# Second RMS norm's root moved behind the up-projection, and the last output pair computed by column halves

## What is computed

```python
def rmsnorm(x, w):
    xf = x.astype(jnp.float32)
    y = xf * lax.rsqrt(jnp.mean(xf * xf, axis=-1, keepdims=True) + EPS)
    return (y * w.astype(jnp.float32)).astype(x.dtype)
...
def conv_glu(h, w_up, conv_w, conv_b, w_down):
    gate, val = jnp.split(jnp.einsum('bsd,df->bsf', h, w_up), 2, axis=-1)
    gate = causal_dwconv(gate, conv_w, conv_b)
    return jnp.einsum('bsf,fd->bsd', jax.nn.gelu(gate, approximate=False) * val, w_down)
...
        x = x + jnp.einsum('bsm,md->bsd', mix, w_out[l])
        h = rmsnorm(x, norm2_w[l])
        x = x + conv_glu(h, ffn_w_up[l], ffn_conv_w[l], ffn_conv_b[l], ffn_w_down[l])
```

## Time and profile before

| | us |
|---|---|
| median of 3 runs | 436.13 |
| lowest and highest run | 435.36 and 436.80 |
| profiled execution, first to last instruction (span) | 434.3 |
| PE busy | 412.1 (95%) |
| DVE busy | 278.3 (64%) |
| ACT busy | 247.6 (57%) |

### The profile page before, as it was taken

The page is one execution under the profiler, slowest core; times in us unless marked ns, Lnnn a source line. Parts: engine busy times, 40 slices in busy tenths (PEclk is TensorE's granted clock), DMA queues, the critical chain, the costliest instruction groups (busy, mean ns, idle before and its releaser), DMA issues.

```text
span 434.3 us, 6756 instructions
## 1 busy us (share of the span) xinstructions
PE 412.1 (95%) x2676; PEld 371.0 (85%) x2676; DVE 278.3 (64%) x382; ACT 247.6 (57%) x322; POOL 31.8 (7%) x24
## 2 busy tenths in 40 slices
PE   1799999999999999989998799999999999999996
PEld 1799999877888888767886799999999999999995
DVE  2769887846756788788544755654654655656543
ACT  5568877693578656887633464444443543544430
POOL 2004445411011000000000000000000000000000
PEclk9999999999999999999999899999999999999999
DMA  7775495555563343224553175555655555655202
GB/s 203 241 254 164 140 337 189 193 193 165 175 221 118 98 161 130 97 103 190 193 160 132 31 260 195 195 194 186 196 159 179 191 172 178 192 190 193 98 0 97
DMA packets 46244, 73.43 MB, mean 169 GB/s; under 512 B 5026, under 2 KB 27790, under 8 KB 46222
## 3 DMA queue, kind: packets, MB, share of 16 engines
q1 hardware_dynamic: 46222, 73.12, 50.3%
HBM read 72.05 MB, written 1.07 MB: 168 GB/s over the span
## 4 chain that ended last, share of the span: by engine, by line
PE 85%; ACT 6%; DVE 3%; SPq 2%; DMA 1%; issue 1%; DVEq 0%; ACTq 0%
PE pj L1091 22%; PE pj L1093 22%; PE pj L1092 22%; PE mx L1091 5%; PE mx L1092 4%; PE mx L1093 4%; PE mx L1137 4%; PE mx L1134 2%; ACT whi L403 2%; SPq L259 1%; DMA wraw<-in_w_in 1%; DVE wlo L715 1%; ACT L531 1%; ACT seg_b L489 1%; ACT sz_b L531 0%
## 5 line engine op out<-in xcount | busy, mean ns | idle before, releaser
L715 DVE TENSOR_TENSOR wlo<-wraw,whi 128x2048 fp32r<-128x2048 f32 x60 | 137.4, 2291 | 100.0 <-ACT whi L403 99.9
L403 ACT CAST whi<-wraw 128x2048 fp32r<-128x2048 f32 x65 | 123.7, 1905 | 108.6 <-PE pj L1093 80.5
L1091 PE MATMUL pj<-hT_hi,whi 128*128 128x256 f32 x512 | 145.9, 285 | 2.3 <-DVE hT_lo L734 2.3
L1092 PE MATMUL pj<-hT_lo,whi 128*128 128x256 f32 x512 | 145.5, 284 | 0.0
L1093 PE MATMUL pj<-hT_hi,wlo 128*128 128x256 f32 x512 | 145.4, 284 | 0.0
L1091 PEld LDWEIGHTS pj<-hT_hi,whi 128*128 128x128 f32 x512 | 98.9, 193 | 3.2 <-DVE wlo L715 1.8
L1092 PEld LDWEIGHTS pj<-hT_lo,whi 128*128 128x128 f32 x512 | 98.9, 193 | 0.4
L1093 PEld LDWEIGHTS pj<-hT_hi,wlo 128*128 128x128 f32 x512 | 98.9, 193 | 0.0
L1091 PE MATMUL pj<-whi,hT_hi 128*128 128x512 f32 x144 | 58.1, 403 | 0.0
L1093 PE MATMUL pj<-whi,hT_lo 128*128 128x512 f32 x144 | 56.3, 391 | 0.0
L1092 PE MATMUL pj<-wlo,hT_hi 128*128 128x512 f32 x144 | 56.1, 390 | 0.0
(11 more groups left out here) (189 smaller groups left out, 421.6 us busy)
## 6 DMA issues: line engine op xcount, KB each, us to landing
wraw<-in_w_in SPq DMA_DIRECT2D x24, 1024.0 KB, 5.2
wraw<-in_ffn_w_up SPq DMA_DIRECT2D x44, 512.0 KB, 4.5
wraw<-in_ffn_w_down SPq DMA_DIRECT2D x11, 1024.0 KB, 4.8
wraw<-in_w_out SPq DMA_DIRECT2D x8, 1024.0 KB, 4.9
seg_b<-ld_rows SPq DMA_DIRECT2D x4, 512.0 KB, 6.2
x_sb<-in_x SPq DMA_DIRECT2D x2, 512.0 KB, 4.0
Wm_b<-m_rows_d SPq DMA_DIRECT2D x1, 512.0 KB, 7.7
out_x<-x_sb SPq DMA_DIRECT2D x1, 512.0 KB, 2.7
```

The lines of the kernel that those rows point to most:

```text
L403: nc.scalar.copy(whi[:, slot, :], wraw[:, slot, :]).then_inc(s.hi_done, 1)
L715: nc.vector.tensor_tensor(wlo[:, slot, :], wraw[:, slot, :], whi[:, slot, :].bitcast(F32), ALU.subtract).then_inc(s.lo_done, 1)
L1091: pe_mm(ps, a_hi, b_hi, start=start, stop=False, skip_group_check=shared)
L1092: pe_mm(ps, a_hi, b_lo, start=False, stop=False, skip_group_check=shared)
```

## The change

The diff leaves out fifteen empty lines at the head of the file (so line numbers of the changed kernel differ), the names of the new semaphores and a slice of `ones` that had become larger.

```diff
...
@@ -91,7 +76,10 @@
         par = sb("par", [P, P + 4 * FC + 2])
         ident = sb("ident", [P, P])
         cmask = sb("cmask", [P, 384])
-        ones = sb("ones", [16, P])
+        ones = sb("ones", [P, P])
+        gr = sb("gr", [P, 2, T])
+        rbc = sb("rbc", [P, T])
+        rdiag = sb("rdiag", [P, NT, P])
         bias3 = sb("bias3", [P, 4])
         expa = sb("expa", [16, 1])
         Dbc = sb("Dbc", [P, SH])
...
@@ -644,13 +632,36 @@
                 split(u + 2)
                 for job, args in jobs.get(u, []):
                     job(*args)
-            row_norm([(s.x2_ready, 1), (s.x2_ready, 2)], s.ssq2, s.ms2, s.rt2, 4, U_FFN + 1)
-            transposed_hi(s.h2_ps, s.h2_hi, hT_hi, p_n2, 4)
+            def x2_square(half, t):
+                act.wait_ge(s.x2_ready, 2 * half + t + 1)
+                cs = slice(half * 512, (half + 1) * 512)
+                nc.scalar.activation(xn[:, t, cs], x_sb[:, t, cs], ACT.Square,
+                                     accum_out=stat[:, 32 + 2 * half + t:33 + 2 * half + t]).then_inc(s.ssq2, 1)
+            def x2_hi(half):
+                for b in (2 * half, 2 * half + 1):
+                    act.wait_ge(s.h2_ps, b + 1)
+                    for i in range(2):
+                        c = 2 * b + i
+                        nc.scalar.activation(hT_hi[:, c, :], bank[b][:, i * T:(i + 1) * T], ACT.Copy,
+                                             scale=par[:, p_n2 + c:p_n2 + c + 1]).then_inc(s.h2_hi, 1)
+            split(U_FFN + 1)
+            x2_square(0, 0)
+            x2_square(0, 1)
+            x2_hi(0)
+            x2_square(1, 0)
+            x2_square(1, 1)
+            act.wait_ge(s.ms2, 1)
+            nc.scalar.activation(stat[:, 36:38], stat[:, 36:38], ACT.Sqrt).then_inc(s.rt2, 1)
+            x2_hi(1)
 
             def gate_base(i, b):
-                act.wait_ge(s.unit_done, up_count(i))
+                act.wait_ge(s.gscaled, i + 1)
                 for k in range(2):
-                    nc.scalar.activation(acc[:, 0, k, :], pj[b][:, k * T:(k + 1) * T], ACT.Identity,
+                    nc.scalar.activation(acc[:, 0, k, :], gr[:, k, :], ACT.Identity,
                                          bias=par[:, bass.ds(i * 2 + (p_fcb + k), 1)],
                                          scale=par[:, bass.ds(i * 2 + (p_fcw + 2 * FC + k), 1)]).then_inc(s.gbase, 1)
 
...
@@ -1024,18 +1035,57 @@
                 for job, args in jobs.get(u, []):
                     job(*args)
 
-            def add_mix(t):
-
-                if t == 0:
-                    dve.wait_ge(s.x2_ps, 1)
+            def add_mix(half, t):
+                if half and t:
+                    dve.wait_ge(s.unit_done, U_FFN)
                 else:
-                    dve.wait_ge(s.unit_done, U_FFN)
-                nc.vector.tensor_tensor(x_sb[:, t, :], x_sb[:, t, :], pj[t][:, :], ALU.add).then_inc(s.x2_ready, 1)
-                dve.wait_ge(s.x2_ready, t + 1)
-
-            row_norm(s.ssq2, s.ms2, s.rt2, s.x2_rows, 4, add_mix)
-            transposed_lo(s.h2_hi, s.h2_lo, hT_hi, hT_lo, p_n2, 4)
+                    dve.wait_ge(s.x2_ps, 2 * half + t + 1)
+                cs = slice(half * 512, (half + 1) * 512)
+                nc.vector.tensor_tensor(x_sb[:, t, cs], x_sb[:, t, cs], pj[t][:, cs], ALU.add).then_inc(s.x2_ready, 1)
+            def x2_lo(half):
+                for b in (2 * half, 2 * half + 1):
+                    dve.wait_ge(s.h2_hi, 2 * b + 2)
+                    for i in range(2):
+                        c = 2 * b + i
+                        nc.vector.scalar_tensor_tensor(out=hT_lo[:, c, :], in0=bank[b][:, i * T:(i + 1) * T],
+                                                       scalar=par[:, p_n2 + c:p_n2 + c + 1], in1=hT_hi[:, c, :].bitcast(F32),
+                                                       op0=ALU.mult, op1=ALU.subtract).then_inc(s.h2_lo, 1)
+            def x2_ms():
+                dve.wait_ge(s.ssq2, 4)
+                link(nc.vector.tensor_tensor(stat[:, 36:38], stat[:, 32:34], stat[:, 34:36], ALU.add))
+                nc.vector.tensor_scalar(stat[:, 36:38], stat[:, 36:38], 1.0 / D, EPS, ALU.mult, ALU.add).then_inc(s.ms2, 1)
+            def x2_root():
+                dve.wait_ge(s.rt2, 1)
+                nc.vector.reciprocal(stat[:, 38:40], stat[:, 36:38]).then_inc(s.r2_ready, 1)
+                dve.wait_ge(s.r2_ready, 1)
+                for t in range(NT):
+                    nc.vector.tensor_scalar(rdiag[:, t, :], ident[:, :], stat[:, 38 + t:39 + t], None, ALU.mult).then_inc(s.rdiag_ready, 1)
+            add_mix(0, 0)
+            add_mix(0, 1)
+            add_mix(1, 0)
+            x2_lo(0)
+            add_mix(1, 1)
             split(U_FFN + 1)
+            x2_ms()
+            x2_lo(1)
+            x2_root()
+            dve.wait_ge(s.rbc_ps, 1)
+            nc.vector.tensor_copy(rbc[:, :], bank[0][:, 0:T]).then_inc(s.rbc_ready, 1)
+            def gate_scale(i, b):
+                dve.wait_ge(s.unit_done, up_count(i))
+                if b == 0:
+                    dve.wait_ge(s.rbc_ready, 1)
+                nc.vector.tensor_tensor(gr[:, :, :], pj[b][:, 0:512].rearrange("p (k t) -> p k t", k=2),
+                                        rbc[:, :].unsqueeze(1).to_broadcast([P, 2, T]), ALU.mult).then_inc(s.gscaled, 1)
 
             def gate_taps(i, b):
                 dve.wait_ge(s.gbase, i * 2 + 2)
@@ -1043,7 +1093,7 @@
                     if back == 2:
                         dve.wait_ge(s.gtap, i * 2 + 2)
                     for k in range(2):
-                        ins = nc.vector.scalar_tensor_tensor(out=acc[:, 0, k, back:T], in0=pj[b][:, k * T:(k + 1) * T - back],
+                        ins = nc.vector.scalar_tensor_tensor(out=acc[:, 0, k, back:T], in0=gr[:, k, 0:T - back],
                                                              scalar=par[:, bass.ds(i * 2 + (p_fcw + FC * (2 - back) + k), 1)],
                                                              in1=acc[:, 0, k, back:T], op0=ALU.mult, op1=ALU.add)
                         if back == 1:
@@ -1061,6 +1111,7 @@
                 nc.vector.tensor_tensor(gT_lo[:, b, :, :], glu, gT_hi[:, b, :, :].bitcast(F32), ALU.subtract).then_inc(s.glo, 1)
 
             def step(i, b, first=False, last=False):
+                gate_scale(i, b)
                 gate_taps(i, b)
                 split(step_unit(i, 2), step_slot(2))
                 gate_mul(i, b)
@@ -1074,13 +1125,15 @@
             for c in range(2):
                 split(step_unit(0, c))
             ffn_steps(dve, step)
+            gate_scale(FJ - 1, (FJ - 1) % 2)
             gate_taps(FJ - 1, (FJ - 1) % 2)
             gate_mul(FJ - 1, (FJ - 1) % 2)
             gate_lo(FJ - 1, (FJ - 1) % 2)
             for k in range(2 * NT):
                 dve.wait_ge(s.last_ps, k + 1)
                 t, cs = k // 2, slice(k % 2 * 512, (k % 2 + 1) * 512)
-                nc.vector.tensor_tensor(x_sb[:, t, cs], x_sb[:, t, cs], mx[t][:, cs], ALU.add).then_inc(s.res_ready, 1)
+                nc.vector.scalar_tensor_tensor(out=x_sb[:, t, cs], in0=mx[t][:, cs], scalar=stat[:, 38 + t:39 + t], in1=x_sb[:, t, cs],
+                                               op0=ALU.mult, op1=ALU.add).then_inc(s.res_ready, 1)
 
 
         @block.tensor
@@ -1092,10 +1145,12 @@
                 pe_mm(ps, a_hi, b_lo, start=False, stop=False, skip_group_check=shared)
                 return pe_mm(ps, a_lo, b_hi, start=False, stop=stop, skip_group_check=shared)
 
-            def channels_first(ps, slot, half, turned=None):
+            def channels_first(ps, slot, half, turned=None, between=None):
 
                 for k in range(4):
                     kk = half * 4 + k
+                    if k == 2 and between:
+                        between()
                     if turned:
                         pe.wait_ge(turned, kk + 1)
                     for c in range(4):
@@ -1405,7 +1460,7 @@
                 else:
                     pe.wait_ge(s.mlT_lo, kc - 12 + 1)
 
-            for i, kc in enumerate(OUT_PAIRS[:-2]):
+            for i, kc in enumerate(OUT_PAIRS[:-1]):
                 u = U_OUT + i
                 lo_ready(pe, u)
                 parts = [mix(kc), mix(kc + 1)]
@@ -1414,37 +1469,56 @@
                 for job, args in jobs.get(u, []):
                     job(*args)
 
-            for t in range(NT):
-                for i in (-2, -1):
-                    kc, u = OUT_PAIRS[i], U_FFN + i
-                    if t == 0:
-                        mix_ready(kc + 1)
-                        lo_ready(pe, u)
-                    for k in range(2):
-                        a_hi, a_lo = mix(kc + k)
-                        for half in range(2):
-                            w = slice(k * 1024 + half * 512, k * 1024 + (half + 1) * 512)
-                            ins = products(pj[t][:, half * 512:(half + 1) * 512], a_hi[:, t * P:(t + 1) * P], a_lo[:, t * P:(t + 1) * P],
 ```

(51 more changed lines are left out.)

## The result

| | before | changed |
|---|---|---|
| median, us | 436.52 (16 runs) | 437.78 (16 runs) |
| lowest and highest | 435.36 and 438.18 | 436.21 and 439.11 |
| ratio, 95% interval | | 1.003 (1.0018 to 1.0042) |
| span of the profiled execution | 434.3 | 436.1 |

The changed kernel is slower by 1.3 us. The interval excludes no change at all, and it lies on both sides of the 0.3% that I had set as the bound of what can be told from no change. It was predicted at 436.3 with a range of 434.9 to 438.4.

What follows compares the result with a forecast made beforehand. PE was taken as the bound, busy 412.1 of 434.3 us. A 0.4 us gain at the boundary and 0.7 lost in the last step sum to +0.3 on 436.13; forecast 436.3, range 434.9 to 438.4.

Steps and rivals of the forecast that it cites:

- The first gap: PE's idle time before unit 32: 1.7 us, with unit 32 starting at 238.9 against 242.23, 3.3 us gained.
- The new wait: Before unit 34: PE waits for VectorE's remainder, made behind the copy of the spread root; about 2.9 us idle.
- The rival without this wait: Before unit 34: PE finds the remainder ready at 251.6 and starts 2.9 us earlier; time 433.4, chance 0.05.
- The boundary with the clock held: From unit 31 to the down-projection of step 0, at full clock: 0.4 us gained.
- The loop: Inner steps: one more 0.68 us DVE multiplication in each of ten, covered by PE's work, costed at nothing.
- The last step: Final step's ACT and DVE chain: the added multiplication has no cover, 0.7 us lost, bounds 0.6 to 0.8.
- The sum and its base: Whole kernel: 0.4 gained at the boundary, 0.7 lost at the end, +0.3 us on the median of 436.13.
- the clock holds: Behind the idle time before unit 34: granted clock stays 1.00; the forecast case, 436.3 us, chance 0.50.
- the clock falls in the new wait: Before unit 34: about 2.9 us idle brings the clock to 0.50, 1.4 us more; time 437.7, chance 0.28.
- within 0.3%: Whole kernel's time: between 434.8 and 437.4 us, not told from no change; chance 0.55.
- The first part: Boundary up to unit 32: the halves gain 3.3 us; rival that they gain nothing taken at 438, chance 0.10.

Runs made afterwards that it cites:

- the 2.0 us gap: Changed kernel plus 6 extra 128x256 matmuls on TensorE between the spread root and unit 34: 437.1 us, ratio 1.0019.
- the 3.4 us gap: Changed kernel plus two more VectorE copies of the spread root, to an unread tile, ahead of the one that counts: 439.48 us, ratio 1.0057.

## Why the prediction came out as it did

**The first gap.** Unit 32 was put 8.2 us behind unit 31's start; it came at 8.12 (238.81 - 230.69), with VectorE's last addition as the releaser. Right, and so was its reason: letting PE go ahead of that addition removed the gap.

**The new wait.** Unit 34 was put at 23.8 us behind unit 31's start and came at 23.92; 2.9 us of idle time were foretold and 2.7 found, for the spread root's two f32 products are recorded as four matmuls and take a little longer. (The parts of the bounds, 0.2 + 0.2 + 2.24 + 0.14, give 2.8 for the lower one, not 2.9.) Its cause, the place of the remainders behind the copy, is shown by the order alone being worth 4.6 us. The rival without this wait was priced at 433.4, and the kernel that takes it away measured 433.44.

**The boundary with the clock held.** Foretold as a gain of 0.4 us; in the execution in which it held it was 0.53 (35.54 from unit 31 to the down-projection, against 36.07).

**The loop.** Costed at nothing; it cost nothing, with twice the work too.

**The last step.** Foretold as 0.7 us with bounds of 0.6 to 0.8; it is 0.80, and 0.06 more for the final additions. Both misses are in the price of operands. The base from SBUF takes 594 ns where it took 554 from PSUM:

```profile
L1083 DVE TENSOR_TENSOR x_sb<-x_sb,mx 128x512 f32<-128x512 f32 x4 | 2.8, 688 | 3.8 <-PE mx L1093 3.8
...
L664 ACT ACTIVATE acc<-gr,par 128x256 f32<-128x256 f32 x22 | 12.0, 594 | 42.4 <-DVE gr L1087 42.4
...
L1135 DVE SCALAR_TENSOR_TENSOR x_sb<-mx,stat,x_sb 128x512 f32<-128x512 f32 x4 | 3.0, 751 | 3.6 <-PE mx L1146 3.6
```

I had argued from the earlier trace rows that no such difference showed, comparing operations of other functions and other scalar operands (495 and 490 ns). The like-for-like pair (L664 here, L653 in the earlier trace rows) shows 40 ns. The Trainium skill ("VectorE: DVE Perf Modes", The TRN2 errata) has formulas for ScalarE that are 52 cycles apart for the two sources, at its 1.2 GHz an estimate of 43 ns. The trace agrees with it, and I had set it aside. The final addition takes 751 ns as a three-operand form with a scalar, against 688 as a sum of two before (L1083, the first line); L734, on which I had relied, is half as wide, and I had compared its pace from start to start and not its duration.

**The sum and its base.** 0.3 more than 436.13 is 436.4, and the bounds of the terms give 435.8 at the lower end; the text has 436.3 and 435.6. The base was itself low: the median of 3 runs was 436.13, that of 16 is 436.52.

**The clock: the step that failed.** I gave "the clock holds" 0.50 and "the clock falls in the new wait" 0.28 and took the first as the forecast. It was the other way round: in 28 of 40 executions with this gap the clock fell. The two cases were priced well, 436.3 and 437.7: the executions that held it lie around 436.6, and the median 437.78 is the rival's time. The range holds the result because it was drawn around both cases; the single number was that of the case that was met less often. The error was to ask which of two gaps in one trace 2.9 us is nearer to, as if there were a length from which the clock falls. With gaps of 2.0, 2.7 and 3.4 us alike some executions kept the clock and some lost it, so one trace could not have told. That also made "within 0.3%" too likely: the result lies on the bound between it and slower.

**The rivals that were not.** The first part did not fail, and the new wait was there. That the halves would gain without the interleaved transposes was not a rival of mine, and the experiment on it was mis-sized by 0.8 us, for a reason given there.

## What to carry to other kernels

A wait put into an in-order engine's program holds up everything written behind it: before adding one, list what follows and who needs that, and write first what is ready and does not depend on it. A gain at one place of a chain that is repaid a few microseconds later shows as "no change" in the time; the list of waits by releaser, before and after, shows both at once. Where a change leaves TensorE idle as long as here (2.0 to 3.4 us), price the clock's fall as a share of the executions, and time several of them.

## What the hardware showed that was not expected

The fall need not come in the gap: in the profiled execution with the 2.0 us gap, the matmuls had run for 1.2 us at full pace when it came. So it was with the transposes not interleaved: unit 34 starts at 255.36, and the matmuls slow down from 0.12 to 0.21 us at 256.53.

```profile
254.28:255.50 1.22, 1.22 (x10) 1.22 (x11) 1.22 (x1) 0.00 (x0) 0.00 (x0) 1.00 0.08 16
255.60:259.00 3.40, 3.40 (x19) 3.40 (x18) 2.24 (x4) 1.94 (x3) 0.00 (x0) 0.50 0.97 300
```

The recorded clock can miss a slow stretch at the start of an execution: in the second profile of the changed kernel the first matmuls of the input projection are 0.21 us apart, the pace of 1.2 GHz, while the stretch shows a granted clock of 1.00; in the profile of the kernel before they are 0.12 apart.

```profile
14.94 0.42 PE L1145 MATMUL pj<-hT_lo,whi 128*128 128x256 f32 x1
15.15 0.41 PE L1146 MATMUL pj<-hT_hi,wlo 128*128 128x256 f32 x1
```

```profile
16.00:18.50 2.50, 2.50 (x14) 2.50 (x14) 1.18 (x4) 0.97 (x1) 0.00 (x0) 1.00 0.64 153
```

In these two it costs little: where the start was quick, PE waits 1.5 us for a small remainder afterwards, where it was slow it does not, and unit 31 starts at 230.7 and 231.0. It can cost more. In the profile with the 3.4 us gap that pace lasts until 20.5, again with a recorded clock of 1.00, and unit 31 starts at 231.58, 0.9 us behind the changed kernel's 230.69:

```profile
20.29 0.41 PE L1146 MATMUL pj<-hT_hi,whi 128*128 128x256 f32 x1
20.50 0.32 PE L1147 MATMUL pj<-hT_lo,whi 128*128 128x256 f32 x1
20.66 0.28 PE L1148 MATMUL pj<-hT_hi,wlo 128*128 128x256 f32 x1
```

```profile
14.40:20.60 6.20, 6.20 (x29) 6.20 (x30) 4.22 (x8) 2.88 (x4) 0.00 (x0) 1.00 0.82 284
```

A start like this would put an execution of the changed kernel about as high as the seven between 438.9 and 439.7; that it is the cause there is not shown.
